# Two stacked transformer blocks on one core: another start of the first block, nine operations in other places, and the forget gates' running sums as split rows

## What is computed

```python
h = rmsnorm(x, norm_mix)                       # start of the program
(fq, fk, fv, ff, gq, gk, gv, ...) = split_projection(h @ w_in)
logf = log_sigmoid(ff + fox_fbias)             # forget gates, 4 heads
c = cumsum(logf, axis=1)
s = q @ k.T * scale + (c[:, :, :, None] - c[:, :, None, :])
p = softmax(where(mask, s, -inf)); ya = p @ v          # "fox" attention
# stick-breaking attention: a = exp(z + rc) @ v
# gated delta rule: triangular systems solved by joining blocks 16, 32, 64
x = x + rmsnorm(y, post_g) * factor            # ends of three phases of block two
```

## Time and profile before

| | |
|---|---|
| three runs | 1159.71, 1161.66 (median), 1163.03 us |
| the profiled execution | 1161.39 us |
| its span | 1159.5 us, so 1.9 us lie around it |
| busy in the span | PE 1143.6 us (99%), DVE 741.9 (64%), ACT 591.2 (51%), POOL 102.2 (9%) |
| DMA | 209.83 MB, 181 GB/s |

### The profile page before, as it was taken

One profiled execution on the slowest core, in us unless ns is written; L12 is line 12 of the kernel. 1 busy time (PEld: TensorE's weight loads), 2 busy tenths in 40 slices (PEclk: granted clock), 3 DMA queues, 4 the chain that ended last, 5 costly groups with the idle time before them and its releaser, 6 DMA issues.

```text
span 1159.5 us, 16582 instructions
## 1 busy us (share of the span) xinstructions
PE 1143.6 (99%) x6478; PEld 998.1 (86%) x6478; DVE 741.9 (64%) x920; ACT 591.2 (51%) x788; POOL 102.2 (9%) x160
## 2 busy tenths in 40 slices
PE   8999999999999999999999999999999999999997
PEld 7998788898888999988888898799888878889885
DVE  5867676657867787863665454565767466544455
ACT  5675544445564765643544443464554365444343
POOL 6410211000011000000000000200500010000011
PEclk9999999999999999999999999999999999999999
...
GB/s 227 216 135 124 182 198 134 129 183 182 207 171 141 224 208 190 174 206 181 166 239 193 170 163 214 152 229 156 147 206 221 160 210 236 187 175 181 208 137 73
DMA packets 123919, 209.83 MB, mean 181 GB/s; under 512 B 10965, under 2 KB 60234, under 8 KB 123851
## 3 DMA queue, kind: packets, MB, share of 16 engines
...
## 4 chain that ended last, share of the span: by engine, by line
PE 90%; DVE 3%; ACT 2%; DMA 2%; issue 1%; POOL 1%; SPq 0%; DVEq 0%; POOLq 0%; ACTq 0%
PE ACCP L852 27%; PE ACCP L854 27%; PE ACCP L853 27%; PE SMP L1037 3%; PE SMP L1030 1%; DVE LO L2131 1%; ACT HI L1569 1%; DMA X<-in_x_dram 1%; DMA RAW<-in_w_in_dram 1%; PE SMP L852 1%; PE SMP L854 0%; PE SMP L853 0%; DVE XS L2176 0%; DMA GAIN_ROW<-in_norm_mix_dram 0%; PE SMP L1200 0%
## 5 line engine op out<-in xcount | busy, mean ns | idle before, releaser
L2131 DVE TENSOR_TENSOR LO<-RAW,HI 128x1024 fp32r<-128x1024 f32 x366 | 437.9, 1233 | 229.9 <-ACT HI L1569 226.5
L1569 ACT ACTIVATE HI<-RAW 128x1024 fp32r<-128x1024 f32 x366 | 370.2, 1054 | 272.7 <-PE ACCP L854 221.5
L852 PE MATMUL ACCP<-HI,XH 128*128 128x512 f32 x688 | 271.2, 394 | 0.5 <-POOL LO L747 0.5
L854 PE MATMUL ACCP<-HI,XL 128*128 128x512 f32 x688 | 268.1, 390 | 0.0
L853 PE MATMUL ACCP<-LO,XH 128*128 128x512 f32 x688 | 267.8, 389 | 0.0
L852 PE MATMUL ACCP<-XH,HI 128*128 128x256 f32 x688 | 195.9, 285 | 0.3 <-POOL LO L771 0.3
L854 PE MATMUL ACCP<-XH,LO 128*128 128x256 f32 x688 | 194.7, 283 | 0.0
L853 PE MATMUL ACCP<-XL,HI 128*128 128x256 f32 x688 | 194.6, 283 | 0.0
L854 PEld LDWEIGHTS ACCP<-HI,XL 128*128 128x128 f32 x688 | 129.1, 188 | 27.4
L852 PEld LDWEIGHTS ACCP<-HI,XH 128*128 128x128 f32 x688 | 129.2, 188 | 26.8 <-POOL LO L747 1.3
L853 PEld LDWEIGHTS ACCP<-LO,XH 128*128 128x128 f32 x688 | 129.3, 188 | 25.7
...
## 6 DMA issues: line engine op xcount, KB each, us to landing
...
```

The lines of the kernel that those rows point to most:

```text
L852: pe.matmul(dst, lhs[0], rhs[0], start=start, stop=False)
L854: return pe.matmul(dst, lhs[1], rhs[0], start=False, stop=stop)
L1569: act.activation(HI[:, n % RING, half_of(half)], RAW[:, n % RAWS, half, :], ACT.Copy).then_inc(hi_ready, 1)
L2131: dve.tensor_tensor(LO[:, s, c], RAW[:, n % RAWS, half, :], HI[:, s, c].bitcast(f32), ALU.subtract).then_inc(lo_ready[s], 1)
```

## The change

- **Start.** The gain is loaded already spread over the partitions, in two halves by SP (one ahead of each half of block 0). Each tile's squares are shared, half on ACT, half on DVE; POOL adds both and takes the root. Scaling, transposes and splits go by feature half first, then by token tile. `first_gemm` does, for each half of the block, all HI times XH, then HI times XL, then LO times XH, with the last transposes inside. All four LO pieces of block 0 are POOL's. POOL's three tiny loads come behind them. The spins are 24, 4 and 4.
- **Running sums.** A product `fcum` makes the four running sums as rows twice, at partitions 0 to 3 and 32 to 35; ACT rounds them all, DVE puts the rest into rows 32 to 35; each head then adds one float32r product of a selecting matrix with these rows. DVE prepares the inputs ahead of `heads_norm`.
- **Moves.** Exp of Z on ACT goes ahead of the squares and of the second half of a split, and all four `stick_arg` stand together on DVE. The T32 copies go ahead of `normalise`; `y_split(2)` goes ahead of half of a split. `f_open` does the eight products of XH of each four k ahead of the four of XL. `post_norm` multiplies by factor and gain first, when the squares are done, and by the root in the second operation.

```diff
-SPIN_ROW, SPIN_SCALED, SPIN_SPLIT = 6, 2, 8
+SPIN_LOAD, SPIN_TURN = 24, 4
...
-SMALL = norm_turns("norm_mix") + ["cols0", "cols1", "cols2", "tinyT", "tiny"]
+MIX_TURNS = [(t, b) for b in range(2) for t in range(NT)]
+SMALL = [f"norm_mix.{t}{b}" for t, b in MIX_TURNS] + ["cols0", "cols1", "cols2", "tinyT", "tiny"]
...
-SMALL += ["Z16_0", "Z16_1", "Tt32_0", "Tt32_1", "fS0", "fS1a", "fS1b", "Z32_0", "Z32_1", "T32_0", "T32_1"]
+SMALL += ["Z16_0", "Z16_1", "fcum", "Tt32_0", "Tt32_1", "fS0", "fS1a", "fS1b", "Z32_0", "Z32_1", "T32_0", "T32_1"]
...
+    for half in range(2):
+        part = slice(half * 512, (half + 1) * 512)
+        sp.dma_start(MIX_GAIN[:, part], A["norm_mix"][:, part].broadcast_to([P, 512])).then_inc(mix_gain_loaded[half], 16)
+        load("gdn", Turn(0), f_block(w["w_in"], C_GQKV), (half,))
...
+            pool.wait_ge(mix_sq, t + 1)
+            pool.wait_ge(sumsq, t + 1)
+            link(pool.tensor_tensor(total, total, MIX_SS[:, t:t + 1], ALU.add))
+            pool.tensor_tensor(ROOT[f"{r}.{t}"], total, MINUS_HALF[:, 0:1], ALU.pow).then_inc(root_ready, 1)
...
+    for half in range(2):
+        for quarter, signal in enumerate((first_lo, lo_ready[0])):
+            if half == 0 and quarter == 0:
+                pool.wait_ge(first_hi, 1)
+            else:
+                pool.wait_ge(hi_ready, half + 1)
+            c = slice(quarter * 512, quarter * 512 + 512)
+            part = slice(half * 1024 + quarter * 512, half * 1024 + quarter * 512 + 512)
+            pool.tensor_tensor(LO[:, 0, part], RAW[:, 0, half, c], HI[:, 0, part].bitcast(f32), ALU.subtract).then_inc(signal, 1)
+    pool.wait_ge(bias_zeroed, 1)
+    pool.dma_start(BROW[:, 0:4], A["fox_fbias"].broadcast_to([P, HEADS])).then_inc(tiny_loaded, 16)
+    pool.dma_start(BROW[:, 8:12], A["gdn_dt_bias"].broadcast_to([P, HEADS])).then_inc(tiny_loaded, 16)
...
+            for weights, x in ((HI, XH), (HI, XL), (LO, XH)):
                 for k in range(4 * half, 4 * half + 4):
-                    if features == 0:
-                        if k == 0:
-                            pe.wait_ge(first_lo, 1)
-                        elif k == 2:
-                            lo_is_ready(pe, "gdn", j, half=0)
-                        elif k == 4:
-                            lo_is_ready(pe, "gdn", j)
-                        ready(k)
-                    c = slice(k * 256 + features * P, k * 256 + features * P + P)
-                    last = three(acc("gdn", j)[:, features * SEQ:(features + 1) * SEQ], (HI[:, 0, c], LO[:, 0, c]),
-                                 (xh[:, k, :], xl[:, k, :]), features == 0 and k == 0, features == 1 and k == KT - 1)
+                    if k % 4 == 0 and weights is HI and x is XH:
+                        pe.wait_ge(norm_hi, 2 * half + 2)
+                        pe.wait_ge(first_hi, 1) if half == 0 else pe.wait_ge(hi_ready, 2)
+                    if k == 2 and weights is HI and x is XH:
+                        pe.wait_ge(hi_ready, 1)
+                    if k % 4 == 0 and x is XL:
+                        for m in range(NT):
+                            small_is_taken(pe, f"norm_mix.{m}{half}")
+                    if k == 0 and weights is LO:
+                        mix_turn(1, 1)
...
+                for b in range(2):
+                    if j == 0:
+                        pe.wait_ge(norm_hi, 4 * NORMS.index(r) + 2 * t + b + 1)
+                    for k in range(4 * b, 4 * b + 4):
+                        c = slice(k * 256, (k + 1) * 256)
+                        pe.matmul(dst, XH[:, k, tok(t)], HI[:, s, c], start=k == 0, stop=False)
+                        pe.matmul(dst, XH[:, k, tok(t)], LO[:, s, c], start=False, stop=False)
+                    if j == 0:
+                        small_is_taken(pe, f"{r}.{t}{b}")
+                    for k in range(4 * b, 4 * b + 4):
+                        c = slice(k * 256, (k + 1) * 256)
+                        last = pe.matmul(dst, XL[:, k, tok(t)], HI[:, s, c], start=False, stop=k == KT - 1)
                 if t == 1:
                     last.then_inc(block_done, 1)
...
+    spin(SPIN_LOAD)
     pe.wait_ge(masks_ready, 1)
-    for t in range(NT):
-        norm_turn("norm_mix", XS, t)
-    spin(SPIN_SPLIT)
+    mix_turn(0, 0)
+    spin(SPIN_TURN)
...
+    pe.wait_ge(cum_in, 1)
+    small_bank_free(pe, "fcum")
+    pe.matmul(small("fcum")[0:36, 0:SEQ], CUM_IN[:, 0, :], flat(UPTO[:, :, :]), start=True, stop=False)
+    finish(pe.matmul(small("fcum")[0:36, P:SEQ], CUM_IN[:, 1, :], TRI, start=False, stop=True))
...
-            last = pe.matmul(dst, TS[:, 0, h:h + 1].broadcast_to([P, P]), flat(UPTO[:, 0:t + 1, :]), start=False,
-                             stop=t == 0 and h == heads[-1])
-            if t == 1:
-                last = pe.matmul(dst[:, P:SEQ], TS[:, 1, h:h + 1].broadcast_to([P, P]), TRI, start=False, stop=h == heads[-1])
+            last = pe.matmul(dst, CUM_SEL[0:36, h, :], CUM[0:36, 0:n], start=False, stop=h == heads[-1])
...
+    mix_split(0, 0)
+    act.wait_ge(raw_ready[0][0], 16)
+    act.activation(HI[:, 0, 0:512], RAW[:, 0, 0, 0:512], ACT.Copy).then_inc(first_hi, 1)
+    mix_split(1, 0)
+    act.activation(HI[:, 0, 512:1024], RAW[:, 0, 0, 512:1024], ACT.Copy).then_inc(hi_ready, 1)
+    mix_split(0, 1)
     split(0, (1,))
+    mix_split(1, 1)
     for n in range(1, RING):
         split(n)
     act.wait_ge(tiny_w_loaded, 16 * 2)
...
-    split_ahead("foxqk", Turn(3))
+    split_ahead("foxqk", Turn(3), (0,))
+    for h in range(HEADS):
+        small_is_taken(act, f"rc{h}")
+    act.activation(Z[:, :, :], Z[:, :, :], ACT.Exp).then_inc(stick_ready, 1)
     for t in range(NT):
         for c in range(2):
             acc_is_taken(act, "foxqk", Turn(c), t)
         act.activation(XS[:, t, :], HT[:, t, :], ACT.Square).then_inc(heads_sq, 1)
+    split_ahead("foxqk", Turn(3), (1,))
     split_ahead("foxv", Turn(0))
-    for h in range(HEADS):
-        small_is_taken(act, f"rc{h}")
-    act.activation(Z[:, :, :], Z[:, :, :], ACT.Exp).then_inc(stick_ready, 1)
...
+    small_is_done(act, "fcum")
+    copy(CUM[0:36, :], small("fcum")[0:36, 0:SEQ], cum_hi)
...
-    dve.wait_ge(lo_ready[0], 1)
-    split(0, (1,))
+        dve.tensor_tensor_reduce(out=XS[:, t, 512:DM], in0=X[:, t, 512:DM], in1=X[:, t, 512:DM], scale=1.0 / DM, scalar=EPS,
+                                 op0=ALU.mult, op1=ALU.add, accum_out=MIX_SS[:, t:t + 1]).then_inc(mix_sq, 1)
+    mix_scale(0, 0)
+    mix_scale(1, 0)
+    mix_scale(0, 1)
+    mix_split(0, 0)
+    mix_split(1, 0)
+    mix_scale(1, 1)
+    mix_split(0, 1)
+    mix_split(1, 1)
...
-    for h in range(2):
+    for h in range(4):
         stick_arg(h)
     split_ahead("foxqk", Turn(3))
-    for h in range(2, 4):
-        stick_arg(h)
+    link(dve.memset(CUM_IN[:, :, :], 0.0))
+    dve.tensor_copy(CUM_IN[:, :, 0:4], TS[:, :, 0:4])
+    dve.tensor_copy(CUM_IN[:, :, 32:36], TS[:, :, 0:4])
+    dve.tensor_tensor(CUM_SEL[0:36, :, :], IDENT[0:36, 0:4].unsqueeze(2).broadcast_to([36, HEADS, P]), IDENT[0:36, 32:36].unsqueeze(2).broadcast_to([36, HEADS, P]), ALU.add).then_inc(cum_in, 1)
...
+    dve.wait_ge(cum_hi, 1)
+    dve.tensor_tensor(CUM[32:36, :], small("fcum")[32:36, 0:SEQ], CUM[32:36, :].bitcast(f32), ALU.subtract).then_inc(bank_of("fcum"), 1)
...
+    for t in range(NT):
+        take_small(f"T32_{t}", ME[:, t], by_head(small(f"T32_{t}")))
     normalise(("fS0",), FP0[:, :, :], 0)
     normalise(("fS1a", "fS1b"), FP1[:, :, :], 4)
-    for t in range(NT):
-        take_small(f"T32_{t}", ME[:, t], by_head(small(f"T32_{t}")))
     split_ahead("gate_a", Turn(0))
...
-    split_ahead("gate_a", Turn(2))
+    split_ahead("gate_a", Turn(2), (0,))
     y_split(2, ("fo0", "fo1"), lambda t: (YH[:, :, tok(t)], YL[:, :, tok(t)], by_head(small(f"fo{t}"))))
+    split_ahead("gate_a", Turn(2), (1,))
...
-        root = root_is_ready(f"{phase}.{m}")
+        dve.wait_ge(post_sq, NT * list(PSS).index(phase) + m + 1)
         dve.wait_ge(post_gain_loaded, 16 * (n + 1))
         sums = flat(ACCP[:, 2 * m:2 * m + 2, :])
-        link(dve.scalar_tensor_tensor(out=sums, in0=sums, scalar=root, in1=POST_GAIN[:, :], op0=ALU.mult, op1=ALU.mult))
-        dve.scalar_tensor_tensor(out=X[:, m, :], in0=sums, scalar=factor, in1=X[:, m, :],
+        link(dve.scalar_tensor_tensor(out=sums, in0=sums, scalar=factor, in1=POST_GAIN[:, :], op0=ALU.mult, op1=ALU.mult))
+        root = root_is_ready(f"{phase}.{m}")
+        dve.scalar_tensor_tensor(out=X[:, m, :], in0=sums, scalar=root, in1=X[:, m, :],
```

98 lines of the change are left out of this document (53 added, 45 removed).

## The result

| | before | changed |
|---|---|---|
| median of 20 runs | 1161.38 us | 1163.27 us |
| lowest to highest | 1159.0 to 1163.03 | 1160.54 to 1167.13 |
| the profiled execution | 1161.39, span 1159.5 | 1164.84, span 1163.1 |
| forecast | | 1156.1 (1152.2 to 1159.0) |

The ratio is 1.0016, with a 95% interval of 1.001 to 1.0022: 1.9 us slower, where 5.3 us less was forecast. The runs of the changed kernel also lie wider apart, 6.6 us against 4.0, and its profiled execution is one of the longer ones, 1.6 above its median. The traces therefore tell where time goes; how much of it a typical execution loses is told by the medians.

The account below looks back on a forecast made before the run. PE was taken as the bound, busy 1143.6 us of 1159.5. Terms -2.6 + 1.6 - 1.85 - 1.2 - 1.5 = -5.55 on 1161.39 gave 1155.8, or 1156.1 against the median; range 1152.2 to 1159.0.

Parts of the forecast that it names:

- The start (-2.6): Program start to block 2: first product near 11.5 instead of 14.41, block 1 2.9 earlier, less 0.3 for block 2's load.
- The exponential (+1.6): Exp of Z to join(16): wait of 1.65 goes, new waits of 1.4 at fTq0 and 1.8 at join(16).
- The rival of the late clock: At the start: idle products don't bring full pace, half pace to about 21 us, start +6.7, 1165.4 us; chance 0.04.
- Running sums (-1.85): Scores: float32 products worth 3.5 removed, selecting products of 0.9 added, so -2.5; fcum adds 0.65.
- T32, T64: At joined(32) and turn_joined(64): PE's waits of 0.77 and 0.39 go, together -1.2.
- f_open: Opening of "up": late start of 0.38 is covered, but PE waits as much longer for DVE's LO; 0, at best -0.4.
- post_norm: End of down1 and mix_o: DVE's first operation no longer waits 0.77 for POOL's root, twice 0.77, -1.5.
- The start's rival: The start gives nothing: all spins slow, or block 2 and 3 loads delayed by POOL's tiny ones; about 1159.3 us, chance 0.14.

Follow-up runs that it names:

- both other forms of the sums: Changed kernel with selecting products after all products of q and k, or spread over all 128 partitions; one execution each, scores 5.23 and 4.22 us.
- the mended kernel with the late copy: Changed kernel with mends on ACT, DVE and the selecting products, but TINY's copy in its old place behind block 4's Silu: 1155.33 us, ratio 0.9946.
- the exchange: Changed kernel with the second half of the split directly behind the exponential of Z on ACT, ahead of the squares: 1161.96 us, ratio 1.0008.
- the move undone: Changed kernel with the exponential of Z and the two late subtractions of rest sums back in their old places: 1160.06 us, ratio 0.999.
- the copy early: Changed kernel with ACT's copy of TINY ahead of the splits of block 8 instead of behind block 4's Silu: 1161.94 us, ratio 1.0006.
- grouped: Changed kernel with each tile's products of q and k first, then all its selecting products; one execution, scores 5.23 us.
- 128 partitions: Changed kernel with running sums spread over all 128 partitions, zeros in the 92 that carry nothing, order unchanged; one execution, scores 4.22 us.

## Why the prediction was wrong

**The start (-2.6): right at its place, wrong at the end.** First product and block 1 stood within 0.7 of the forecast. The first step that failed is the one that looked only for block 2's load as the next limit, and let the rest of the gain stand to the end of the kernel. The next limit on PE's path was the copy of TINY at 52, at the end of a chain of DVE's convolutions and ACT's Silus that runs from 28 on at its own pace. In the kernel before, PE arrived when the copy was just done (52.08 and 51.94), and so no wait stood in the earlier trace rows or anywhere else to warn of it. The start alone gave 0.6 us, not 2.6, and its interval doesn't exclude nothing. The prediction followed the delay down the chain for the exponential, but not the gain for the start. Within the start, the spins ran slow until 6.2 and ended at 9.3, not at 8.4: their slow part was taken from the length of the gain's stretch, and no run ties the one to the other.

**The exponential (+1.6): right mechanism, too small.** fTq0 waited 3.0 instead of 1.4. DVE was late by 5.9 instead of 3.0: about 2.9 by the move itself, as worked out, and 3.1 because the first half of that split was late already, its load being issued at 127.27 instead of 124.17. Of this, 1.8 is the lateness that the chain ahead had from the wait for TINY; the other 1.3 stays open. With the tiny loads early, where that lateness is absent, the reductions are 3.6 late and PE waits 2.6. PE's own lateness at this point (0.0 at so0) gave no cover. At join(16) the wait for FQK was too large in the forecast: 0.3 and 0.7 instead of 1.8, because PE itself came late by the half pace.

**What a wait costs.** This was in no term: the sum counted a wait at its length, and that is the second step that failed. A wait of 2 to 3 us, or two shorter ones close together, can be followed by a stretch of half pace: 1.5 us at 53 to 58, about 1.7 at 156 to 160. It doesn't happen every time. Behind the wait at TINY the clock fell in the changed kernel (2.75), with the old sums (wait 2.2), in both other forms of the sums (2.3 and 2.0) and in the mended kernel with the late copy (2.35), and not in the start alone (2.25), the exchange (2.24) or with the move undone (1.8). Behind the wait at fTq0 it fell in the changed kernel (3.0), with the copy early (2.9) and grouped (2.3), and not with the tiny loads early (2.6) or 128 partitions (2.4). The changed kernel's twenty executions have a mean granted clock of 0.996, 86 executions of the kernel before 0.998. By these means (0.9960 and 0.9982, of readings to three places) I estimate that a typical execution loses 2.6 us more to the lower clock than before. The rival of the late clock had the mechanism at the wrong place: at the start the full pace came 3.3 earlier than before.

**Running sums (-1.85): wrong by 2.9.** This is the third step that failed: the bounds of 0.06 to 0.22 for a selecting product were taken from products of 128 partitions. It measured 0.25 and 0.31, and made its neighbour 0.2 dearer, so the scores gained nothing (+0.3 instead of -2.5); fcum was near its price (0.77 for 0.65). With 128 partitions the term is right.

**T32, T64, f_open, post_norm:** forecast -1.2, 0, -1.5; measured -1.4, -0.1, -1.8. The LO that took back f_open's gain is in the trace:

```profile
379.66 0.38 PE L1019 MATMUL SMP<-HI,XH 128*128 128x256 f32 x1 [0.48 <-DVE LO L2183]
```

**Rivals.** None described what happened. The start's rival named the right place to doubt but the wrong cause: the tiny loads moved the time about, they didn't make it. The range ended 4.3 below the measured time; the sum's terms were each bounded by their own neighbourhood, and no term stood for a chain further on that had no slack.
